# Expert mixture kernel: the first unit's dots taken between steps of the second unit's selection, and tile 1's first query products placed among the gathers

## The reference

```python
def peer(h, w_pq, sub_keys, u_emb, v_emb):
    q = (h @ w_pq).reshape(B, S, PEER_HEADS, 2, PEER_DHALF)
    sc = jnp.einsum("bshcd,hcnd->bshcn", q, sub_keys)
    s_top, i_top = lax.top_k(sc, PEER_TOPK)
    cand = s_top[..., 0, :, None] + s_top[..., 1, None, :]
    cand_idx = i_top[..., 0, :, None] * N_KEYS + i_top[..., 1, None, :]
    ...
    best, pos = lax.top_k(cand, PEER_TOPK)
    expert_idx = jnp.take_along_axis(cand_idx, pos, axis=-1)
    gate = jax.nn.softmax(best, axis=-1)
    ...
    a = jax.nn.gelu(jnp.einsum("ced,cd->ce", u_emb[idx], hx), approximate=False)
    return jnp.einsum("ce,ced->cd", g * a, v_emb[idx])
```

## Time and profile before

| what | value |
|---|---|
| median of 3 runs | 1680.86 us (1677.45 to 1682.59) |
| profiled execution | 1683.13 us, its span 1680.7 us |
| PE, DVE, ACT, POOL busy | 88%, 60%, 37%, 19% of the span |
| software DMA queue (gathers and POOL's others) | 279.18 MB |
| first and last dot of the mixture | 313.0 and 983.1 us |

### The profile page before, as it was taken

How to read it: one execution, slowest core, us unless ns; L and a number is a source line. 1 busy time by engine, 2 the same in 40 slices (tenths; PEclk the granted TensorE clock), 3 DMA queues, 4 the chain that set the end, 5 groups by cost and what they waited for, 6 DMA issues and landing times.

```text
span 1680.7 us, 16573 instructions
## 1 busy us (share of the span) xinstructions
PE 1478.8 (88%) x5970; PEld 1009.9 (60%) x5970; DVE 1013.1 (60%) x1959; ACT 625.4 (37%) x1292; POOL 313.4 (19%) x297
## 2 busy tenths in 40 slices
PE   6999999799977876887987779989999989899998
PEld 5868898555442332333333237767887869778876
DVE  3997776675767766777775443435555455654553
ACT  1014482233333332533333224453444345534442
POOL 1000000243433444444444300400000000000000
PEclk9999999899999999999999989899999999999999
DMA  7345544899999999999999936222544435054541
GB/s 306 126 150 146 99 152 151 346 407 391 412 420 420 420 420 416 391 416 413 411 415 418 421 148 230 78 84 101 200 182 169 175 142 189 34 199 157 195 175 76
DMA packets 51761, 428.55 MB, mean 255 GB/s; under 512 B 6632, under 2 KB 6776, under 8 KB 9568
## 3 DMA queue, kind: packets, MB, share of 16 engines
q0 software_dynamic: 40464, 279.18, 41.7%
q1 hardware_dynamic: 11216, 148.33, 23.3%
HBM read 422.49 MB, written 4.98 MB: 254 GB/s over the span
## 4 chain that ended last, share of the span: by engine, by line
PE 62%; DMA 18%; DVE 11%; ACT 5%; issue 2%; POOL 0%; DVEq 0%; SPq 0%; ACTq 0%; POOLq 0%
DMA pool<-uv,experts 17%; PE psum L722 17%; PE psum L1067 11%; PE psum L842 10%; PE psum L843 10%; PE psum L844 10%; PE psum L755 3%; DVE pool L1995 3%; PE psum L799 2%; DVE ring_lo L1649 2%; DMA ring<-stream 1%; ACT w_hi L1248 1%; ACT xn L1168 1%; ACT diag L1480 1%; ACT L1470 1%
## 5 line engine op out<-in xcount | busy, mean ns | idle before, releaser
L1067 PE MATMUL psum<-pool,diag 128*128 128x512 f32 x1024 | 484.7, 623 | 124.4 <-ACT diag L1480 116.0
L1995 DVE CUSTOM_DVE_ANT_0 pool<-pool,xn 128x1024 f32<-128x1024 f32 x256 | 313.5, 1226 | 210.0 <-DMA pool<-uv,experts 207.9
L1067 PEld LDWEIGHTS psum<-pool,diag 128*128 128x128 f32 x1024 | 194.5, 197 | 404.1 <-issue 205.0
L679 POOL DMA_INDIRECT pool<-uv,experts x256 | 283.5, 1107 | 529.8 <-PE psum L1067 373.0
L1649 DVE TENSOR_TENSOR ring_lo<-ring,w_hi 128x2048 fp32r<-128x2048 f32 x76 | 172.4, 2290 | 108.2 <-ACT w_hi L1248 108.2
L722 PE MATMUL psum<-hT,ring 128*128 128x256 f32 (+1 forms) x832 | 175.3, 372 | 2.9 <-DVE hT L1580 1.0
L842 PE MATMUL psum<-w_hi,h_hi 128*128 128x512 f32 x400 | 162.6, 406 | 9.9 <-DVE ring_lo L1649 8.1
L1248 ACT ACTIVATE w_hi<-ring 128x2048 fp32r<-128x2048 f32 x76 | 142.7, 1907 | 68.6 <-DMA ring<-stream 38.5
L722 PEld LDWEIGHTS psum<-hT,ring 128*128 128x128 f32 x832 | 152.2, 197 | 25.2 <-issue 4.8
L843 PE MATMUL psum<-ring_lo,h_hi 128*128 128x512 f32 x400 | 158.5, 396 | 0.0
L844 PE MATMUL psum<-w_hi,h_lo 128*128 128x512 f32 x400 | 157.4, 393 | 0.0
(11 more groups left out here) (267 smaller groups left out, 2008.9 us busy)
## 6 DMA issues: line engine op xcount, KB each, us to landing
ring<-stream SPq DMA_DIRECT2D x66, 2048.0 KB, 7.6
pool<-uv,experts POOLq DMA_INDIRECT x256, 12.5
ring<-stream SPq DMA_DIRECT2D x3, 1024.0 KB, 4.7
t_scratch<-tab POOLq DMA_DIRECT2D x1, 2048.0 KB, 56.5
rpb_scratch<-tab POOLq DMA_DIRECT2D x1, 1792.0 KB, 22.4
ring<-stream SPq DMA_DIRECT2D x1, 1792.0 KB, 7.0
row<-rows POOLq DMA_DIRECT2D x1, 1672.0 KB, 15.3
ring<-stream SPq DMA_DIRECT2D x1, 1664.0 KB, 6.5
```

Source lines behind the costliest of these rows:

```text
L679: gp.indirect_dma_start(out=gath[:, n % NROWS, :], out_offset=None, in_=uv, in_offset=bass.IndirectOffsetOnAxis(ap=experts[:, n:n + 1], ax ...
L1067: last = nc.tensor.matmul(psum[:, RB + half, :], diag[:, n % NDIAG, :], gath[:, n % NROWS, D + 512 * half:D + 512 * half + 512], start=k = ...
L1995: ins = V.tensor_tensor_reduce(out=row_u, in0=row_u, in1=xn[:, n // SLOTS, :], scale=1.0, scalar=0.0, op0=ALU.mult, op1=ALU.add, accum_out ...
```

## The change

Five things. (1) DVE's selection of unit 1: step 0 goes ahead of tile 1's norm, step 1 between the norm and the two copies of its transposes, and steps 2 to 8 each behind one of the dots 0 to 6. Unit 2's steps follow dots 8 to 15 (before: 7 to 15). (2) The tile 1 query products of heads 0 and 1 go from ahead of slot 0 to slots 13 and 15, their scores to slot 17. (3) Each query product of heads 2 to 7 is done in two halves (8 MATMULs each), two slots apart. (4) The exponential of unit 1's gates goes from ahead of the first pair to behind pair 5. (5) The PSUM fill numbers and the copy's wait conditions follow the new order; so does the weight stream, since the chunk of heads 6 and 7 waits for `("pqt", 1, 1)`, now at slot 15.

```diff
-QUERY_SLOTS = {1: ("pq", 2), 3: ("sc", 2), 8: ("pq", 3), 11: ("sc", 3), 18: ("pq", 4), 21: ("sc", 4),
...
-SELECT_FIRST_AT = (7, 8, 9, 10, 11, 12, 13, 14, 15)
+QUERY_SLOTS = {1: [("pq", 2, 0)], 3: [("pq", 2, 1)], 5: [("sc", 2)], 7: [("pq", 3, 0)], 9: [("pq", 3, 1)], 11: [("sc", 3)],
+               13: [("pqt", 0, 1)], 15: [("pqt", 1, 1)], 17: [("sct", 0, 1), ("sct", 1, 1)],
...
+FIRST_STEPS = {k: [(1, k + 2)] for k in range(7)}
+FIRST_STEPS.update({8: [(2, 0)], 9: [(2, 1)], 10: [(2, 2)], 11: [(2, 3)], 12: [(2, 4)], 13: [(2, 5)], 14: [(2, 6)],
+                    15: [(2, 7), (2, 8)]})
...
             tile_transposes("N2", 1, xn[:, 1, :])
             wait_tile("N2", 1)
-            for head in range(2):
-                tile_query(head, 1)
-            for head in range(2):
-                tile_scores(head, 1)
...
+            def query_half(head, j):
+                dst = bank(("pq", head)) if j else begin(("pq", head))
+                w = wait_chunk(pe, ("pq", head // 2))[:, 0:4096].rearrange("p (k n) -> p k n", k=KD)
+                c = 2 * P * (head % 2) + P * j
+                last = accumulate(dst[:, S * j:S * j + S], [(w[:, k, c:c + P], hT[:, k, :]) for k in range(KD)])
+                if j:
+                    last.then_inc(bank_filled, 1)
...
-                    if n in QUERY_SLOTS:
-                        query(*QUERY_SLOTS[n])
+                    for step in QUERY_SLOTS.get(n, ()):
+                        query(step)
...
+            def query_copy(step):
+                kind, head = step[:2]
+                if kind == "pqt":
+                    act.wait_ge(bank_filled, FILL_NO["sc", head + 2] + 1)
+                    tile_query_copy(head, 1)
+                elif kind == "sct":
+                    tile_score_copy(head, 1)
...
             gate_exp(0)
-            for head in range(2):
-                tile_query_copy(head, 1)
-            for head in range(2):
-                tile_score_copy(head, 1)
-            gate_exp(1)
...
+                    for item in QUERY_SLOTS.get(n, ()):
+                        query_copy(item)
+                if pair == 5:
+                    gate_exp(1)
...
             add_tile(1, 1)
-            second_norm(1)
+            select_step(1, 0)
+            second_norm(1, lambda: select_step(1, 1))
             weights(0)
-            for k in range(SELECT_STEPS):
-                select_step(1, k)
             for unit in range(UNITS):
                 for k in range(TOPK):
                     dot(TOPK * unit + k)
-                    at = SELECT_AT if unit else SELECT_FIRST_AT
-                    if unit + 2 < UNITS and k in at:
-                        select_step(unit + 2, at.index(k))
+                    if unit == 0:
+                        for step in FIRST_STEPS.get(k, ()):
+                            select_step(*step)
+                    elif unit + 2 < UNITS and k in SELECT_AT:
+                        select_step(unit + 2, SELECT_AT.index(k))
```

More of the change, by code:

```diff
@@ L153, in fm_fills, with query_fill @@
     return [(name, i, pair) for i in range(chunks) for pair in range(2)]
-QUERY_SLOTS = {1: ("pq", 2), 3: ("sc", 2), 8: ("pq", 3), 11: ("sc", 3), 18: ("pq", 4), 21: ("sc", 4),
-               28: ("pq", 5), 31: ("sc", 5), 40: ("pq", 6), 43: ("sc", 6), 52: ("pq", 7), 55: ("sc", 7)}
-SELECT_FIRST_AT = (7, 8, 9, 10, 11, 12, 13, 14, 15)
+QUERY_SLOTS = {1: [("pq", 2, 0)], 3: [("pq", 2, 1)], 5: [("sc", 2)], 7: [("pq", 3, 0)], 9: [("pq", 3, 1)], 11: [("sc", 3)],
+               13: [("pqt", 0, 1)], 15: [("pqt", 1, 1)], 17: [("sct", 0, 1), ("sct", 1, 1)],
+               19: [("pq", 4, 0)], 21: [("pq", 4, 1)], 23: [("sc", 4)], 27: [("pq", 5, 0)], 29: [("pq", 5, 1)],
+               31: [("sc", 5)], 39: [("pq", 6, 0)], 41: [("pq", 6, 1)], 43: [("sc", 6)], 51: [("pq", 7, 0)],
+               53: [("pq", 7, 1)], 55: [("sc", 7)]}
+FIRST_STEPS = {k: [(1, k + 2)] for k in range(7)}
+FIRST_STEPS.update({8: [(2, 0)], 9: [(2, 1)], 10: [(2, 2)], 11: [(2, 3)], 12: [(2, 4)], 13: [(2, 5)], 14: [(2, 6)],
+                    15: [(2, 7), (2, 8)]})
+def query_fill(step):
+    return step[:2] if step[0] == "pq" else step
 TOKEN_CHUNKS = (("va", 0), ("cqkv", 0), ("cqkv", 1))
@@ L178, in fill_list @@
     out += [("pqt", 0, 0), ("sct", 0, 0), ("pqt", 1, 0), ("wout", 1, 1), ("sct", 1, 0), ("N2", 1, 0), ("N2", 1, 1)]
-    out += [("pqt", 0, 1), ("pqt", 1, 1), ("sct", 0, 1), ("sct", 1, 1)]
-    out += QUERY_SLOTS.values()
+    out += [query_fill(step) for steps in QUERY_SLOTS.values() for step in steps if step[0] != "pq" or step[2]]
     for t in range(NT):
@@ L1029, in _, with query @@
             wait_tile("N2", 1)
-            for head in range(2):
-                tile_query(head, 1)
-            for head in range(2):
-                tile_scores(head, 1)
-            def query(kind, head):
-                dst = begin((kind, head))
-                if kind == "pq":
[L1038 to L1041, removed]
+            def query_half(head, j):
[5 more added lines that the diff above has]
+                    last.then_inc(bank_filled, 1)
+            def query(step):
+                kind, head = step[:2]
+                if kind == "pq":
+                    query_half(head, step[2])
+                elif kind == "pqt":
+                    tile_query(head, 1)
+                elif kind == "sct":
+                    tile_scores(head, 1)
                 else:
+                    dst = begin((kind, head))
                     wait_emptied(pe, ("pq", head))
@@ L1048, in query @@
                                                     keys[:, 2 * head + c, :], start=True, stop=True)
-                last.then_inc(bank_filled, 1)
+                    last.then_inc(bank_filled, 1)
             for t in range(NT):
@@ L1420, in _ @@
             split_high(-1, WOUT + 3)
-            def query_copy(kind, head):
-                if kind == "pq":
-                    before = ("sc", head - 2) if head >= 4 else ("sct", head - 2, 1)
+            def query_copy(step):
+                kind, head = step[:2]
+                if kind == "pqt":
+                    act.wait_ge(bank_filled, FILL_NO["sc", head + 2] + 1)
+                    tile_query_copy(head, 1)
+                elif kind == "sct":
+                    tile_score_copy(head, 1)
+                elif kind == "pq":
+                    if step[2] == 0:
+                        return
+                    before = ("sc", head - 2) if head >= 6 else ("sct", head % 2, head // 2 - 1)
                     act.wait_ge(bank_filled, FILL_NO[before] + 1)
@@ L1482, in _ @@
                 for n in (2 * pair, 2 * pair + 1):
-                    if n in QUERY_SLOTS:
-                        query_copy(*QUERY_SLOTS[n])
+                    for item in QUERY_SLOTS.get(n, ()):
+                        query_copy(item)
+                if pair == 5:
+                    gate_exp(1)
                 if k == TOPK // 2 - 1 and unit + 2 < UNITS:
@@ L1925, in add_tile, with second_norm @@
                 V.tensor_tensor(d, d, b, ALU.add).then_inc(emptied_sem(("wout", i, t)), 1)
-            def second_norm(t):
+            def second_norm(t, meanwhile=None):
                 dve.wait_ge(root_ready, roots_before["N2"] + t + 1)
@@ L1931, in second_norm @@
                 V.scalar_tensor_tensor(xn[:, t, :], x[:, t, :], r, row_("norm2"), ALU.mult, ALU.mult).then_inc(xn_ready, 1)
+                if meanwhile is not None:
+                    meanwhile()
                 for hf in range(2):
```

## The result

The changed kernel takes 1685.04 us (median of 20 runs, 1680.71 to 1687.74), the kernel before 1679.41 us (20 runs, 1674.51 to 1684.2): 1.0032 of it, 95% interval 1.0022 to 1.0043. It is 5.6 us slower; the interval is 3.7 to 7.2 us. The forecast was 1685.0, from a median of 1680.86. The profiled execution took 1685.69 us (span 1683.3), where 1687.2 was expected.

What follows compares the result with a forecast made beforehand. DMA engines were taken to bound the mixture's stage: 12.1 us lost against 8.8 before, 3.3 more, plus 0.8 for the clock, makes 4.1 us slower, 1680.9 to 1685.0. Own range 1682 to 1688; 8 of 10, 1678.5 to 1690.

Steps and rivals of the forecast that it cites:

- The bound: Mixture's stage: DMA engines are full; holes in the first 27 slots lose 8.5 us, the most the change can win there.
- The early start: Ahead of slot 0: DVE's first dot comes earlier, so slot 0 starts at 312.4 in place of 317.9, 5.5 us earlier.
- The halves: Query products of heads 2 to 7: halves keep PE from blocking 7 us at a time; no term of their own.
- second hole: DMA windows from 380 and 384: 3 us lost before, at a gather waiting for slot 18; forecast to be gone.
- The work in the slots: PE through slot 13, with tile 1's product: slot 13 spent at 363.2; DMA loses 12.1 us, 3.3 more than before.
- The clock behind the wait: PE's lower clock after its waits on ACT: 0 to 1.7 us on top, 0.8 taken.
- The wait on ACT: Ahead of slot 12: PE waits for diagonals behind unit 1's exponential and table loads; 3.0 us taken, 1.5 to 4.4 possible.
- The second wait covered: Ahead of slot 16: the same wait again, covered by two chunks, 10 us of transfers, with 1.1 us to spare.
- C: Rival, clearly slower: both waits on ACT drop the clock, 6.5 us, 1687.4; decides if slot 21 is spent after 393.2; chance 0.20.
- The late chunk: Weight chunk not asked for until slot 15: row 7 could land at 322, not 327; two chunks then come together.
- A: Rival, the holes close: early start and halves let PE keep up, up to 8.5 us less lost, 1672.4; chance 0.08.
- B: Rival, nothing changes: without the wait ahead of slot 12 the loss is 9.1 against 8.8 us, 1681.2; chance 0.17.

Runs made afterwards that it cites:

- e5: The changed kernel with the query products of heads 2 to 7 whole again, all else as changed: 1683.6 us, ratio to before 1.0017.
- e4: The kernel before with query products of heads 2 to 7 in halves and unit 2's selection steps behind dots 8 to 15: 1675.7 us, ratio 0.9978.
- e1: The changed kernel with unit 1's exponential moved to pair 4, ahead of ACT's wait for PE: 1681.9 us, ratio to before 1.0025.
- e7: The changed kernel with one more table change there and back behind unit 1's exponential in pair 5: 1686.5 us, ratio to before 1.0042.
- e10: e1 with a spare-column gelu behind the exponential, so the gelu table load also precedes ACT's wait: 1679.6 us, ratio to before 0.9994.
- e11: e10 with unit 2's exponential and its gelu load in pair 7, ahead of the copy of tile 1's second product: 1678.9 us, ratio 0.9996.
- e2: The changed kernel with tile 1's two query products back ahead of slot 0, their scores at slot 2: 1671.9 us, ratio to before 0.9953.
- e9: e2 with the weight chunk of heads 6 and 7 held until head 4's product is done (slot 21): 1678.9 us, ratio to before 0.9996.
- e6: The kernel before with the weight chunk of heads 6 and 7 held until head 3's product is done (slot 8): 1685.6 us, ratio 1.0038.
- e8: e2 with the products of heads 2 to 7 whole and tile 1's scores at slot 1: 1672.0 us, ratio to before 0.9947.

## Why the prediction was right

- **The bound.** The time follows the lack of DMA work in the first slots: with twelve kernels the stretch of gathers and the time go together. Right.
- **The early start.** Slot 0 forecast at 312.4, measured 312.13; first dot at 305.63. Right.
- **The halves.** I gave them no term of their own and let the second hole close. It did, but e5, with whole products, lacks only 0.8 us behind 380 too, so in the changed kernel it isn't the halves that close it. That they win 4 us alone (e4) I had not seen: there the loss is one of blocks, not of PE's sum.
- **The work in the slots.** Slot 13 forecast spent at 363.2 plus 0.8 us of clock, measured 364.5 (gather 21 at 364.79). That it came so near is in part luck, since two terms were off in opposite directions. Head 2's product took 3.74 + 3.62 = 7.4 us where 8.3 were put; in e1, e7, e10 and e11, which are the same up to there, it took 8.1 to 8.2. The clock behind the wait cost 2.0 us on slot 12 and 1.1 on the product, 3.1 where I had 0 to 1.7 and took 0.8. The term that was mis-sized is the clock. Its range was read from one case, and the profiles show how far it varies behind the same wait of 2.96 us: nothing in e2, 3.1 us in the changed kernel.
- **The wait on ACT.** 2.96 us, forecast 3.0; with its clock it is, within the interval, all of the loss (e10). The Trainium skill, page "ScalarE: Activation LUTs", says in "Table sets: the hidden batching unit" to do all functions of one set before the next. The traces bear that out: the two added loads made the wait. In "What ACT_TABLE_LOAD costs" it puts a drain beside each load. The traces don't show it: four loads in e7, each with its activation, took 1.28 us each, and the activation started 1.3 us behind the load's start.
- **The second wait covered.** 2.81 us ahead of slot 16. Not settled: no effect shows in the times (e11), but 1.6 to 1.8 us show in the one profile. Slot 21 was spent at 394.3 us, past the 393.2 at which C was to decide, but row 21 too was 2 us later than in the sum, and with it the time at which row 29 was due.
- **The late chunk.** It was in the sum as the 5 us by which row 7 and all behind it could land earlier; e9 gives 7. Alone, in e6, I was wrong: I counted a chunk only as DMA work, not as something that keeps rows from PE.
- **The rivals.** A had what e2 shows: the holes do close when PE's work stays in front, and the time was foreseen (1672.4); against it stood the order that the change had chosen. That e2's 1671.9 lies so near is chance, as A was computed for another kernel. B is what e10 is: without the wait the change is neutral (1681.2 forecast for it, 1679.6 measured beside a before of 1680.2).

That the forecast of 1685.0 was met to 0.04 us is luck. The loss was 5.6 us (3.7 to 7.2), where 4.1 was forecast, and the longer series puts the kernel before at 1679.41, 1.45 us below the median that I started from; the two cancel. By the dots, row 21 of the changed kernel was 14.3 us behind its time without any loss (371.26 against 357) and row 26 of before 9.8 (389.29 against 379.5): 4.5 us more, near the 4.8 of the stretch of gathers. I had also said that this measurement can't tell 5 us from no change; with 20 runs of each kernel it can.

## What to carry to other kernels

Where a queue of transfers is the bound and a ring of buffers feeds it, add up the consumer's work from the start of the stage and compare it with the transfers' due times: the last buffer that comes late sets most of the loss, and what is saved ahead of it may count for nothing (the halves in e5). Work that lies in the idle time ahead of the stage was free here; moved among the consumer's steps, with the transfer that its data's last use holds back (a weight chunk), it cost 13 us, of which 6 came back when the wait that it had brought into the open was hidden. When on ScalarE one function is moved among others of another table, both loads have to be ahead of the wait: the one that switches back stays with the next user unless something calls it up.

## What the runs showed that I had not expected

- Two weight chunks that come together, 4.2 MB, kept the gathers back for nearly as long as both took: DVE waited 10.43 us for row 16 in e6, and 8.70 us for row 23 in the changed kernel. The gathers in flight didn't share evenly with them: of the 5.19 MB moved from 372 to 384 us in the changed kernel they got 1.54, of the 1.47 MB from 352 to 356 us in e6 0.12.
- The same wait of PE, 2.96 us behind busy stretches of much the same work, left the granted clock at 1.00 in e2 and e8 and came with some 6.8 us at 0.50 in the changed kernel. Each is one profile; what decides between them stays open. A wait of 5.99 us (e7) had no longer low stretch than that.
